# A two-block transformer kernel: the norm factor's broadcast earlier, the modulation's products later, first sums in PSUM

## The chip, the cores and the metric

The kernel runs on one core of a Trainium2 chip. The metric is the device time of one execution in microseconds (us). TensorE is called PE in the rows, VectorE DVE, ScalarE ACT, GpSimd POOL; SP issues the DMAs of the weights.

## The reference

x has 512 tokens of 1024 features, in fp32. Two blocks run one after the other. Each is a feed-forward part (2816 wide, gated with silu), a token mixer, and a second feed-forward part. What matters here is the first part of the first block, and the modulation that the second block takes from a vector c:

```python
def _rmsnorm(x, g):
    y = x * rsqrt(mean(x * x, axis=-1) + EPS)
    return y * g
h = _rmsnorm(x, ffn1_norm);  x = x + 0.5 * _swiglu(h, ffn1_w_gate, ffn1_w_up, ffn1_w_down)
h = _rmsnorm(x, mix_norm);   proj = h @ w_in            # then attention and retention on proj
...
h = _rmsnorm(x, ffn2_norm);  x = x + 0.5 * _swiglu(h, ffn2_w_gate, ffn2_w_up, ffn2_w_down)
# second block, before its first sublayer:
mod = silu(c) @ w_ada + b_ada                           # 1024 x 9216
```

## The kernel before

**Layout and units.** x is kept feature-major: 8 tiles of 128 features x 512 tokens. All weights come in one stream of units, each of 128 x 1024 fp32, through a ring of four (`raw`). ACT makes the rounded high part of a unit (`act_split`, L223), POOL the low part (`pool_split`, L230), into `split`, also a ring of four. TensorE takes three matmuls for each 128x128 tile, high by high, high by low, low by high (`three_passes`, L243): 24 matmuls for a unit. A unit is split up to three units ahead of TensorE (LOOKAHEAD) and loaded up to four ahead of its split. A semaphore `unit_used` counts units that TensorE has finished, `unit_lo` units that POOL has split.

**Late norm.** Three norms, those before a.ffn1, a.in and a.ffn2, are "late": the matmuls run on x times the gain, and the factor 1/rms of each token is applied to the result. While the first units run, the squares of x are added up over the 8 tiles (ACT squares at L584, DVE adds at L577). TensorE then sums over partitions with one-column matmuls (`pe_mean_square`, L254, 16 matmuls), ACT takes the root (L290), DVE the reciprocal (L304) and a diagonal (L284), TensorE spreads it over all partitions (`pe_rows`, L279), and ACT copies that "factor" to SBUF (L298). DVE multiplies each finished bank by it (L535 and L544 in the FFN, L716 in the projection). Four PSUM banks serve the units of a group of four, so the first unit of the next group waits until the first bank has been scaled.

**The projection a.in.fm** has five groups of four units, numbered here 0 to 19; unit 4 is the first of the second group. Beside it, DVE makes the modulation: w_ada comes in 8 chunks of 8 tiles (128 x 1152). For each tile DVE multiplies by an entry of silu(c) and adds into one accumulator (`dve_ada`, first tile of a chunk L816, the others L819). TensorE sums each finished chunk over partitions with 9 fp32 matmuls, each of two passes, so 18 in the trace (`pe_ada`, L834), and DVE adds the bias (L825). The next chunk's first product waits for those sums.

**SP's order.** Weight units and w_ada tiles are issued by SP's one queue, in the order of the code (L785 to L804, with ADA_TILES = ((0, 1, 2), (3, 4, 5), (6, 7), ())). The ring for w_ada has four slots. So tile 4 waits until tile 0 has been added, and everything behind it in SP's program waits too:

```python
            if tile >= 4:
                nc.sync.wait_ge(sem("ada_added"), tile - 3)
...
            for u in range(4):
                self.sp_unit(name, t, u)
                if u > 1:
                    self.sp_ada(chunk0 + t, u - 2)
            for u in (2, 3):
                self.sp_ada(chunk0 + t, u)
```

For the first group that gives: units 0, 1, 2, tiles 0, 1, 2, unit 3, tiles 3 to 7, then units 4, 5, 6, tiles 8 to 10, unit 7, tiles 11 to 15, unit 8. Every wait is written out by hand; `meet` (L193) is a barrier of the engines between stages. The functions that the change touches follow, with what calls them.

Of the kernel before, what the change touches and what calls it, by code (L numbers as in the profile page):

```python
# [11 lines left out]
ALU = mybir.AluOpType  # L12
# [7 lines left out]
KD = D // P  # L20
# [9 lines left out]
LOOKAHEAD = 3  # L30
# [34 lines left out]
class Signals:  # L65
# [7 lines left out]
    def sem(self, name):  # L73
        if name not in self.sems:
            self.sems[name] = self.stack.enter_context(self.nc.semaphore(name))
        return self.sems[name]

    def to(self, name, *event, by=1):
        self.count[name] = self.count.get(name, 0) + by
        assert (name, event) not in self.made, (name, event)  # L80
        self.made[name, event] = self.count[name]
        return by

    def at(self, name, *event):
        if self.known is None:
            return 1
        return self.known[name, event]


class Kernel:  # L90
# [354 lines left out]
    def pe_ffn(self, pre, in_front=None):  # L445

        nc, sem, to, at = self.nc, self.sem, self.to, self.at
        late = pre in self.LATE
        free = ("gate_scaled", "up_scaled") if late else ("silu", "act_mul")
        first, last = self.plan[pre + ".up"]["unit"], self.plan[pre + ".up"]["n"] - 1  # L450
        for t, u, g in self.units(pre + ".up"):
            if t > 0:
                nc.tensor.wait_ge(sem(free[u % 2]), at(free[u % 2], pre, t - 1, u // 2))
            elif in_front:
                nc.tensor.wait_ge(sem("resid"), at("resid", in_front, 4 + u))
            nc.tensor.wait_ge(sem("unit_lo"), g + 1)
            for j in range(KD):
                if g == first:
                    self.pe_hs_ready(pre, j)
                mm = self.three_passes(self.ps[:, u, :], slice(j * P, (j + 1) * P), self.hs[:, 0, j, :],  # L460
                                       self.hs[:, 1, j, :], g % RING, j == 0, j == KD - 1)
            mm.then_inc(sem("unit_used"), 1)
            if late and g == first + 1 + (pre == "a.ffn1"):
                self.pe_mean_square(pre)
            if late and g == first + 3:
                self.pe_rows(pre, 7, self.rs)
        for t, u, g in self.units(pre + ".down"):
            mt, part = u // 3, u % 3
            if part == 0 and t == 0:
                nc.tensor.wait_ge(sem(free[mt % 2]), at(free[mt % 2], pre, last, mt // 2))  # L470
            if part == 0 and t > 0:
                nc.tensor.wait_ge(sem("resid"), at("resid", pre, (t - 1) * 4 + mt))
            nc.tensor.wait_ge(sem("unit_lo"), g + 1)
            k0 = sum(DOWN_TILES[:part])
            for j in range(DOWN_TILES[part]):
                if t == 0 and mt == 0:
                    nc.tensor.wait_ge(sem("act_lo"), at("act_lo", pre, (k0 + j) // 2, (k0 + j) % 2))
                mm = self.three_passes(self.ps[:, mt, :], slice(j * P, (j + 1) * P), self.a_s[:, 0, k0 + j, :],
                                       self.a_s[:, 1, k0 + j, :], g % RING, k0 + j == 0, k0 + j == KF - 1)
            mm.then_inc(sem("unit_used"), 1)  # L480
# [184 lines left out]
    def pe_fm_tile(self, g, bank, src, k_from=0, k_n=KD, ready=None):  # L665
# [4 lines left out]
                                   src[1][:, j, :], g % RING, j == 0, j == k_n - 1)  # L670
        return mm

    def pe_fm_project(self, name, n, hook=None):
        nc, sem, to, at = self.nc, self.sem, self.to, self.at
        late = n in self.LATE
        for t, u, g in self.units(name):
            if t > 0:
                e = "fm_dve" if late or u % 2 == 1 else "fm_act"
                nc.tensor.wait_ge(sem(e), at(e, name, t - 1, u))
            elif late:  # L680
                nc.tensor.wait_ge(sem("resid"), at("resid", "a.ffn1", 4 + u))
            nc.tensor.wait_ge(sem("unit_lo"), g + 1)
            self.pe_fm_tile(g, u, self.h_parts, ready=n if t == 0 and u == 0 else None).then_inc(sem("unit_used"), 1)
            if late and t == 0 and u == 1:
                self.pe_mean_square(n)
            if late and t == 0 and u == 3:
                self.pe_rows(n, 7, self.rs)
            if hook and u == 3:
                hook(t)

    def act_fm_project(self, name, dst, late=False):
        nc, sem, to, at = self.nc, self.sem, self.to, self.at
        for t, u, g in self.units(name):
            if not (late and t == 0 and u in (1, 2)):
                self.act_split(g + LOOKAHEAD)
            if late and t == 0 and u == 0:
                self.act_split(g + LOOKAHEAD + 1)
                self.act_rstd("a.in")
                self.act_split(g + LOOKAHEAD + 2)
                self.act_rs("a.in", self.rs_in[:, :])  # L700
            if not late and u % 2 == 0:
                nc.scalar.wait_ge(sem("unit_used"), g + 1)
                nc.scalar.activation(dst[:, 4 * t + u, :], self.ps[:, u, :], ACT.Copy).then_inc(
                    sem("fm_act"), to("fm_act", name, t, u))

    def dve_fm_project(self, name, dst, hook=None, late=False):
        nc, sem, to, at = self.nc, self.sem, self.to, self.at
        if late:
            hook(0, 0)
            hook(0, 1)  # L710
            self.dve_rstd("a.in", self.col_in)
            nc.vector.wait_ge(sem("rs"), at("rs", "a.in"))
        for t, u, g in self.units(name):
            if late:
                nc.vector.wait_ge(sem("unit_used"), g + 1)
                nc.vector.tensor_tensor(dst[:, 4 * t + u, :], self.ps[:, u, :], self.rs_in[:, :], ALU.mult).then_inc(  # L716
                    sem("fm_dve"), to("fm_dve", name, t, u))
            elif u % 2 == 1:
                nc.vector.wait_ge(sem("unit_used"), g + 1)
                nc.vector.tensor_copy(dst[:, 4 * t + u, :], self.ps[:, u, :]).then_inc(  # L720
                    sem("fm_dve"), to("fm_dve", name, t, u))
            if hook and not (late and t == 0 and u < 2):
                hook(t, u)

    def pe_tm_project(self, name, width, hook=None):
# [1411 lines left out]
            self.act_square(n, j, self.x[:, j, :])  # L2137

    def dve_start(self):
        nc, sem, to = self.nc, self.sem, self.to  # L2140
        n, gain = "a.ffn1", self.vec(0)
        nc.vector.memset(self.ones[:, :], 1.0)
        nc.vector.memset(self.eps, EPS)
        nc.vector.memset(self.ssq[:, :], 0.0).then_inc(sem("ssq"), to("ssq", n, -1))
        nc.vector.wait_ge(sem("vecs_landed"), 16)
        for j in range(KD):
            if j % 2 == 0:
                nc.vector.wait_ge(sem(f"x_landed{j // 2}"), 16)
            self.dve_late_lo(n, gain, j)
        for j in range(KD):  # L2150
            self.dve_into_ssq(n, j)
        nc.vector.wait_ge(sem("ident_landed"), 16)

    def act_tables(self, *tables):
# [429 lines left out]
```

## Time and profile before

| what | value |
|---|---|
| median of 3 runs | 2935.22 us (2931.61 to 2938.62) |
| the profiled execution | 2931.5 us |
| its span | 2930.2 us |
| mean granted TensorE clock | 0.949 of full |
| TensorE matmul busy | 2707.9 us, 92% |
| weight unit loads (512 KB), median from issue to landing | 3.4 us |
| w_ada tile loads (576 KB), the same | 5.8 us |

The profile is one execution, taken by the hardware. Its span runs from the first to the last recorded instruction. Rows of a timeline merge equal instructions that follow each other: start, length of the merged stretch, engine, line, tiles, count, and in brackets how long the engine was idle before and what ended that. A matmul counts as busy until its modelled end, so a busy TensorE is not one at its peak.

### The profile page before, as it was taken

Reading aid. Unit: us, or ns where it says so; the run is one execution under the profiler, and the core shown is the slowest. Engines: PE = TensorE matmul, PEld = TensorE weight load, DVE = VectorE, ACT = ScalarE, POOL = GpSimd, SP = SyncE. Lnnn points to the kernel's source line nnn. Section 1 sums busy time; section 2 is a strip of 40 time slices with the busy share of each in tenths; the row PEclk is TensorE's granted clock in tenths of the full one; section 3 lists DMA queues with packets and bytes.
Section 4 is the critical chain, followed back from the end, with each engine's and each line's share of the span. In section 5 each row is a group of like instructions: output and inputs, shape, how many; then the busy total and the mean of one; then the engine's idle time right before and its main releaser. Section 6 shows DMA issues by size and latency. Waiting matters only on the chain.

```text
span 2930.2 us, 30093 instructions
## 1 busy us (share of the span) xinstructions
PE 2707.9 (92%) x12126; PEld 2159.6 (74%) x12126; DVE 868.3 (30%) x1425; ACT 931.4 (32%) x1497; POOL 1270.0 (43%) x645
## 2 busy tenths in 40 slices
PE   8999999975699899999999999998977699899998
PEld 7888878744466688788888788887855487788886
DVE  4222146543666311322211311102026423311101
ACT  4233211202455422332322322223246423322221
POOL 4444434412477344444444444444433344444443
PEclk9999999976799999999999999998989799899999
DMA  4222257712000122222322223231210022132321
GB/s 157 95 99 90 90 206 281 267 40 73 7 1 1 65 94 94 87 94 94 100 93 95 79 94 97 91 96 62 94 49 1 6 96 86 52 100 95 98 92 61
DMA packets 75754, 261.48 MB, mean 89 GB/s; under 512 B 9184, under 2 KB 10464, under 8 KB 75616
## 3 DMA queue, kind: packets, MB, share of 16 engines
q1 hardware_dynamic: 72368, 255.45, 26.3%
q10 hardware_dynamic: 3248, 4.12, 0.5%
q8 instruction: 96, 1.57, 0.2%
q14 instruction: 42, 0.34, 0.0%
HBM read 257.44 MB, written 2.10 MB: 89 GB/s over the span
## 4 chain that ended last, share of the span: by engine, by line
PE 66%; DVE 4%; POOL 3%; ACT 2%; issue 1%; DMA 0%; ACTq 0%; POOLq 0%; DVEq 0%
PE ps L243 57%; POOL prob L1419 2%; PE ps L254 1%; PE ps L1218 1%; PE ps L1575 1%; PE ps L1188 1%; PE ps L1175 1%; PE ps L1176 0%; PE ps L1540 0%; PE ps L279 0%; POOL prob_d L1866 0%; PE ps L1564 0%; ACT hs L431 0%; PE ps L1225 0%; PE ps L1541 0%
## 5 line engine op out<-in xcount | busy, mean ns | idle before, releaser
L230 POOL TENSOR_TENSOR split_ring<-raw_ring,split_ring 128x1024 fp32r<-128x1024 f32 x416 | 1006.2, 2422 | 1301.8 <-ACT split_ring L223 1301.7
L243 PE MATMUL ps<-hs,split_ring 128*128 128x512 f32 x6240 | 1439.6, 392 | 34.8 <-DVE hs L333 8.9
L243 PEld LDWEIGHTS ps<-hs,split_ring 128*128 128x128 f32 x6240 | 1179.9, 189 | 293.4 <-issue 14.7
L223 ACT ACTIVATE split_ring<-raw_ring 128x1024 fp32r<-128x1024 f32 x416 | 437.2, 1052 | 559.6 <-PE ps L243 393.0
L243 PE MATMUL ps<-ffn_act,split_ring 128*128 128x512 f32 x2112 | 495.4, 396 | 0.0
L243 PEld LDWEIGHTS ps<-ffn_act,split_ring 128*128 128x128 f32 x2112 | 397.8, 188 | 97.0
L512 ACT ACTIVATE ffn_act<-tmp 128x512 fp32r<-128x512 f32 x88 | 55.6, 632 | 385.2 <-DVE tmp L548 385.2
L1419 POOL TENSOR_SCALAR prob<-prob,small 128x512 f32<-128x512 f32 (+3 forms) x128 | 140.4, 1115 | 59.7 <-DVE small L1463 59.7
L548 DVE TENSOR_TENSOR tmp<-ps,tmp 128x512 f32<-128x512 f32 x44 | 30.4, 691 | 380.6 <-PE ps L243 380.6
L243 PE MATMUL ps<-split_ring,hs 128*128 128x512 f32 (+1 forms) x480 | 106.1, 384 | 10.3 <-POOLq L196 7.9
L243 PEld LDWEIGHTS ps<-split_ring,hs 128*128 128x128 f32 x480 | 88.9, 197 | 26.5 <-POOLq L196 8.1
L819 DVE SCALAR_TENSOR_TENSOR ada_acc<-ada_w,c_silu,ada_acc 128x1152 f32<-128x1152 f32 x56 | 88.3, 1578 | 9.2 <-DMA ada_w<-in_w_ada 4.8
L544 DVE TENSOR_TENSOR tmp<-ps,sq 128x512 f32<-128x512 f32 x44 | 30.4, 690 | 184.4 <-PE ps L243 184.4
L551 DVE TENSOR_TENSOR ffn_act<-tmp,ffn_act 128x512 fp32r<-128x512 f32 x88 | 64.5, 733 | 61.4 <-ACT ffn_act L512 61.4
L617 DVE SCALAR_TENSOR_TENSOR x<-ps,x 128x512 f32<-128x512 f32 x24 | 16.6, 691 | 221.9 <-PE ps L243 221.9
L633 DVE TENSOR_SCALAR y_over_hs<-ps,coef 128x512 f32<-128x512 f32 x16 | 12.0, 750 | 224.7 <-ACT sq L584 224.7
L2062 DVE TENSOR_TENSOR tmp<-tmp,ps 128x512 f32<-128x512 f32 x32 | 21.3, 684 | 186.1 <-PE ps L243 186.1
L1218 PE MATMUL ps<-turned,vg 128*64 128x512 f32 (+3 forms) x256 | 73.9, 442 | 0.7 <-ACT turned L1376 0.7
L1368 ACT ACTIVATE prob<-ps,small 128x512 f32<-128x512 f32 (+3 forms) x128 | 65.7, 529 | 20.2 <-DVE small L1446 13.3
L509 ACT ACTIVATE tmp<-ps 128x512 f32<-128x512 f32 x44 | 26.3, 598 | 131.6 <-PE ps L243 131.5
L509 ACT ACTIVATE tmp<-tmp 128x512 f32<-128x512 f32 x44 | 27.8, 632 | 123.6 <-DVE tmp L535 123.6
L535 DVE TENSOR_TENSOR tmp<-ps,sq 128x512 f32<-128x512 f32 x44 | 30.4, 690 | 114.7 <-PE ps L243 97.5
(294 smaller groups left out, 2451.7 us busy)
## 6 DMA issues: line engine op xcount, KB each, us to landing
raw_ring<-in_wstream SPq DMA_DIRECT2D x380, 512.0 KB, 3.4
ada_w<-in_w_ada SPq DMA_DIRECT2D x64, 576.0 KB, 5.8
raw_ring<-in_wstream SPq DMA_DIRECT2D x32, 384.0 KB, 3.0
x<-in_x_t SPq DMA_DIRECT2D x4, 512.0 KB, 6.6
decay<-in_decay ACTq DMA_DIRECT2D x4, 512.0 KB, 3.6
out_t<-x SPq DMA_DIRECT2D x8, 256.0 KB, 2.0
raw_ring<-in_wstream SPq DMA_DIRECT2D x4, 304.0 KB, 5.8
cos_r<-in_cos_r ACTq DMA_DIRECT2D x1, 256.0 KB, 3.6
```

What stands on the lines that cost most here:

```text
L223: nc.scalar.activation(self.split[:, s, 0, :], self.raw[:, s, :], ACT.Copy).then_inc(self.sem("unit_hi"), 1)
L230: nc.gpsimd.tensor_tensor(self.split[:, s, 1, :], self.raw[:, s, :], self.split[:, s, 0, :].bitcast(F32), ALU.subtract).then_inc(self.sem( ...
L243: mm = self.nc.tensor.matmul(out, lhs, rhs, start=first and j == 0, stop=last and j == 2)
L509: nc.scalar.activation(self.tmp[:, f, :], gate, ACT.Silu).then_inc(sem("silu"), to("silu", pre, t, f))
L512: nc.scalar.activation(self.a_s[:, 0, 2 * t + f, :], self.tmp[:, 2 + f, :], ACT.Copy).then_inc(sem("act_hi"), to("act_hi", pre, t, f))
L535: nc.vector.tensor_tensor(self.tmp[:, f, :], self.ps[:, u, :], self.rs, ALU.mult).then_inc(sem("gate_scaled"), to("gate_scaled", pre, t, f))
L544: nc.vector.tensor_tensor(up, self.ps[:, u, :], self.rs, ALU.mult).then_inc(sem("up_scaled"), to("up_scaled", pre, t, f))
L551: nc.vector.tensor_tensor(self.a_s[:, 1, 2 * t + f, :], self.tmp[:, 2 + f, :], self.a_s[:, 0, 2 * t + f, :].bitcast(F32), ALU.subtract).th ...
L819: i = nc.vector.scalar_tensor_tensor(self.ada_acc[:, :], w, self.c_silu[:, j:j + 1], self.ada_acc[:, :], ALU.mult, ALU.add)
L1218: mm = nc.tensor.matmul(self.ps[64 * g:64 * g + 64, 7, kb * P:T], self.vg[:, kb, 2 * kind + g, 0:DH], self.pt_n[:, kind, (self.PT_AT + P) ...
L1368: e = nc.scalar.activation(self.prob_n[:, kind, dst:dst + n], self.ps[:, i, col:col + n], ACT.Exp, bias=self.small[:, k:k + 1], scale=-1.0 ...
L1419: s = nc.gpsimd.tensor_scalar(x, x, self.small[:, 16 + k:17 + k], None, ALU.mult)
```

## The change

- In both late FFN stages the factor's broadcast (`pe_rows`) stands behind the third unit instead of the fourth. In a.ffn1 the mean square stands behind the second unit instead of the third; in a.ffn2 it already did.
- In a.in.fm the broadcast stands behind the third unit too. The sums of chunk 0 stand behind unit 5 (group 1, u = 1) instead of unit 3, those of chunk 1 behind unit 8 instead of unit 7; from chunk 2 on nothing changes.
- DVE's first six products no longer stand ahead of the reciprocal; each follows the scaling of its own unit, behind the factor.
- ACT splits units 4 and 5 behind the root and the factor's copy, one with each unit, instead of ahead of them.
- At the start of a.ffn1 the running sum of squares is in PSUM bank 6; only the last add writes to SBUF.

```diff
--- before.py
+++ after.py
@@ -460,9 +460,9 @@
                 mm = self.three_passes(self.ps[:, u, :], slice(j * P, (j + 1) * P), self.hs[:, 0, j, :],
                                        self.hs[:, 1, j, :], g % RING, j == 0, j == KD - 1)
             mm.then_inc(sem("unit_used"), 1)
-            if late and g == first + 1 + (pre == "a.ffn1"):
+            if late and g == first + 1:
                 self.pe_mean_square(pre)
-            if late and g == first + 3:
+            if late and g == first + 2:
                 self.pe_rows(pre, 7, self.rs)
         for t, u, g in self.units(pre + ".down"):
             mt, part = u // 3, u % 3
@@ -670,6 +670,8 @@
                                    src[1][:, j, :], g % RING, j == 0, j == k_n - 1)
         return mm
 
+    ADA_LATER = {(1, 1): 0, (2, 0): 1}
+
     def pe_fm_project(self, name, n, hook=None):
         nc, sem, to, at = self.nc, self.sem, self.to, self.at
         late = n in self.LATE
@@ -683,20 +685,19 @@
             self.pe_fm_tile(g, u, self.h_parts, ready=n if t == 0 and u == 0 else None).then_inc(sem("unit_used"), 1)
             if late and t == 0 and u == 1:
                 self.pe_mean_square(n)
-            if late and t == 0 and u == 3:
+            if late and t == 0 and u == 2:
                 self.pe_rows(n, 7, self.rs)
-            if hook and u == 3:
+            if hook and late and (t, u) in self.ADA_LATER:
+                hook(self.ADA_LATER[t, u])
+            if hook and u == 3 and not (late and t < 2):
                 hook(t)
 
     def act_fm_project(self, name, dst, late=False):
         nc, sem, to, at = self.nc, self.sem, self.to, self.at
         for t, u, g in self.units(name):
-            if not (late and t == 0 and u in (1, 2)):
-                self.act_split(g + LOOKAHEAD)
+            self.act_split(g + LOOKAHEAD)
             if late and t == 0 and u == 0:
-                self.act_split(g + LOOKAHEAD + 1)
                 self.act_rstd("a.in")
-                self.act_split(g + LOOKAHEAD + 2)
                 self.act_rs("a.in", self.rs_in[:, :])
             if not late and u % 2 == 0:
                 nc.scalar.wait_ge(sem("unit_used"), g + 1)
@@ -706,8 +707,6 @@
     def dve_fm_project(self, name, dst, hook=None, late=False):
         nc, sem, to, at = self.nc, self.sem, self.to, self.at
         if late:
-            hook(0, 0)
-            hook(0, 1)
             self.dve_rstd("a.in", self.col_in)
             nc.vector.wait_ge(sem("rs"), at("rs", "a.in"))
         for t, u, g in self.units(name):
@@ -719,7 +718,7 @@
                 nc.vector.wait_ge(sem("unit_used"), g + 1)
                 nc.vector.tensor_copy(dst[:, 4 * t + u, :], self.ps[:, u, :]).then_inc(
                     sem("fm_dve"), to("fm_dve", name, t, u))
-            if hook and not (late and t == 0 and u < 2):
+            if hook:
                 hook(t, u)
 
     def pe_tm_project(self, name, width, hook=None):
@@ -2137,18 +2136,22 @@
             self.act_square(n, j, self.x[:, j, :])
 
     def dve_start(self):
-        nc, sem, to = self.nc, self.sem, self.to
+        nc, sem, to, at = self.nc, self.sem, self.to, self.at
         n, gain = "a.ffn1", self.vec(0)
         nc.vector.memset(self.ones[:, :], 1.0)
         nc.vector.memset(self.eps, EPS)
-        nc.vector.memset(self.ssq[:, :], 0.0).then_inc(sem("ssq"), to("ssq", n, -1))
+        nc.vector.memset(self.ps[:, 6, :], 0.0).then_inc(sem("ssq"), to("ssq", n, -1))
         nc.vector.wait_ge(sem("vecs_landed"), 16)
         for j in range(KD):
             if j % 2 == 0:
                 nc.vector.wait_ge(sem(f"x_landed{j // 2}"), 16)
             self.dve_late_lo(n, gain, j)
-        for j in range(KD):
-            self.dve_into_ssq(n, j)
+        for j in range(KD - 1):
+            nc.vector.wait_ge(sem("squared"), at("squared", n, j))
+            nc.vector.wait_ge(sem("ssq"), at("ssq", n, j - 1))
+            total = self.ps[:, 6, :]
+            nc.vector.tensor_tensor(self.ssq[:, :] if j == KD - 2 else total, self.sq[:, j % 2, :], total,
+                                    ALU.add).then_inc(sem("ssq"), to("ssq", n, j))
         nc.vector.wait_ge(sem("ident_landed"), 16)
 
     def act_tables(self, *tables):
```

`sp_ada` and `sp_ada_stage` are the same in both kernels.

## Rows read from the trace of the kernel before

**Rows 1.** The page, part 1: busy time of each engine, share of the span, instructions.
```profile
PE 2707.9 (92%) x12126; PEld 2159.6 (74%) x12126; DVE 868.3 (30%) x1425; ACT 931.4 (32%) x1497; POOL 1270.0 (43%) x645
```

**Rows 2.** Timeline of a.ffn1's start: start, us, engine, line, what, [idle before <-releaser].
```profile
13.33 5.21 POOL L230 TENSOR_TENSOR split_ring<-raw_ring,split_ring 128x1024 fp32r<-128x1024 f32 x2 [5.11 <-ACT split_ring L223]
...
15.08 7.98 DVE L577 TENSOR_TENSOR ssq<-ssq,sq 128x512 f32<-128x512 f32 x7 [1.67 <-ACT sq L584]
...
19.91 0.63 ACT L584 ACTIVATE sq<-x 128x512 f32<-128x512 f32 x1 [0.16 <-DVE ssq L577]
...
26.93 0.95 PE L254 MATMUL ps<-ones,ssq 128*128 128x1 f32 x8
...
34.20 1.02 PE L279 MATMUL ps<-sq,ones 128*128 128x512 f32 x2
...
36.63 23.68 PE L243 MATMUL ps<-hs,split_ring 128*128 128x512 f32 x103 [1.41 <-DVE tmp L535]
...
42.38 7.64 POOL L230 TENSOR_TENSOR split_ring<-raw_ring,split_ring 128x1024 fp32r<-128x1024 f32 x3 [9.88 <-ACT split_ring L223]
...
45.25 0.68 DVE L535 TENSOR_TENSOR tmp<-ps,sq 128x512 f32<-128x512 f32 x1
...
48.61 1.95 DVE L548 TENSOR_TENSOR tmp<-tmp 128x512 f32<-128x512 f32 x1
```

**Rows 3.** Timeline of a.ffn2's first units.
```profile
1258.89 0.69 DVE L284 TENSOR_TENSOR sq<-ident,tiny 128x512 f32<-128x512 f32 x1
...
1271.65 28.63 PE L243 MATMUL ps<-hs,split_ring 128*128 128x512 f32 x125 [1.41 <-DVE tmp L535]
```

**Rows 4.** Timeline of a.in.fm, its first four units and the first sums.
```profile
382.00 0.82 DVE L816 TENSOR_SCALAR ada_acc<-ada_w,c_silu 128x1152 f32<-128x1152 f32 x1 [1.47 <-DMA ada_w<-in_w_ada]
383.57 2.94 DVE L819 SCALAR_TENSOR_TENSOR ada_acc<-ada_w,c_silu,ada_acc 128x1152 f32<-128x1152 f32 x2 [0.75 <-DMA ada_w<-in_w_ada]
...
390.70 11.17 PE L243 MATMUL ps<-hs,split_ring 128*128 128x512 f32 x48
391.39 1.46 SPq L208 DMA_DIRECT2D raw_ring<-in_wstream  x3
...
396.61 1.06 ACT L223 ACTIVATE split_ring<-raw_ring 128x1024 fp32r<-128x1024 f32 x1 [9.29 <-DMA raw_ring<-in_wstream]
397.57 0.24 ACT L290 ACTIVATE tiny<-ps,tiny 128x4 f32<-128x4 f32 x1
397.75 5.17 POOL L230 TENSOR_TENSOR split_ring<-raw_ring,split_ring 128x1024 fp32r<-128x1024 f32 x2 [7.97 <-ACT split_ring L223]
...
402.77 0.60 ACT L298 ACTIVATE rs_in<-ps 128x512 f32<-128x512 f32 x1 [3.79 <-PE ps L279]
...
409.52 4.00 PE L834 MATMUL ps<-ones,ada_acc 128*128 128x1 f32 x18 [6.79 <-DVE ada_acc L819]
```

**Rows 5.** Timeline of a.in.fm around unit 8; the first line from a shorter stretch.
```profile
427.57 1.41 DVE L819 SCALAR_TENSOR_TENSOR ada_acc<-ada_w,c_silu,ada_acc 128x1152 f32<-128x1152 f32 x1
...
426.96 0.69 DVE L716 TENSOR_TENSOR pqr<-ps,rs_in 128x512 f32<-128x512 f32 x1 [0.98 <-PE ps L243]
...
429.38 1.38 SPq L208 DMA_DIRECT2D raw_ring<-in_wstream  x3
...
436.43 7.06 POOL L230 TENSOR_TENSOR split_ring<-raw_ring,split_ring 128x1024 fp32r<-128x1024 f32 x3 [19.22 <-ACT split_ring L223]
...
437.64 2.06 PE L834 MATMUL ps<-ones,ada_acc 128*128 128x1 f32 x18
...
463.71 22.05 PE L243 MATMUL ps<-hs,split_ring 128*128 128x512 f32 x96 [0.20 <-POOL split_ring L230]
```

**Rows 6.** PE by stretch: us, busy (instructions), granted clock, DMA share, GB/s.
```profile
413.40:418.40 5.00, 5.00 (x13) 0.50 0.15 59
...
515.40:520.80 5.40, 5.40 (x21) 0.50 0.64 207
...
537.60:541.30 3.70, 3.70 (x9) 0.50 0.53 166
```

## The prediction

> **What bounds the kernel now.** I read the page first: TensorE is busy for 2707.9 of 2930.2 us [rows 1], so time moves only where TensorE waits, does extra work, or runs at its lower clock. Then PE's waits in the stages that the diff touches, then their timelines, where the same waits stand in brackets. They show three places:
>
> - In a.ffn1 the broadcast of the factor (L279) stands behind unit 3, the stage's fourth. Rows end at 35.22, ACT copies them, DVE scales the first bank, and only then may TensorE take unit 4: it sits idle 1.41 us before 36.63 [rows 2].
> - a.ffn2 has the same gap, 1.41 us before 1271.65 [rows 3].
> - In a.in.fm the broadcast ends at 402.7 and the first modulation sums (L834) wait 6.8 us for DVE's products, then take 4.00 us for 18 matmuls where the same 18 take 2.06 later [rows 4, 5]. The granted clock, which had been full, was 0.50 (1.2 of 2.4 GHz) in 413.4:418.4 [rows 6], after that idle time. Unit 4 starts at 413.4.
>
> The reader should also see two chains here. ACT's square root at 397.57 comes 7 us after the mean square, since it is queued behind the split of unit 4, whose data landed at 396.6 [rows 4]. And SP is one ordered queue: unit 4's load, issued at 391.39 [rows 4], stands behind the load of product tile 7, which waits until tile 3 has been added. Unit 8's load likewise stands behind tile 15, which waits for tile 11.
>
> **The change, part by part.** One unit of 24 matmuls is a quarter of the 22.05 us that 96 took at 463.71: 5.5 us [rows 5].
>
> *First sums in PSUM, mean square behind the second unit (a.ffn1).* TensorE had used 17.8 us for three units up to 26.9; unit 2 takes 5.5 of it, so unit 1 ends at 21.4. The sums must be done by then. Before, the seven adds ran from 15.08 to 23.06 [rows 2]. Squares and adds alternate at one per 0.79 us when nothing disturbs them (0.63 and 0.16 idle [rows 2]). The first adds fell beside POOL's splits (13.33 to 18.54): at the undisturbed pace the seventh would have ended near 20.4. An operation that reads PSUM took 0.68 at 45.25 with POOL splitting from 42.38 to 50.02 [rows 2]. If the new adds are like that, squares 2 to 7 run at 0.79 from 15.85 and end at 20.4: no wait. If they pace as before, TensorE waits until 23.1, 1.7 us. I take none, by the row at 45.25, which is the nearest in form. The memset of a PSUM bank stands where the other stood, at DVE's idle start: nothing. The Trainium skill ("SBUF — State Buffer", section "SBUF: two separate sides") says that VectorE and GpSimd hold a shared port pair for a whole instruction when the VectorE one has two SBUF inputs; this trace agrees (the multiplication of two SBUF tiles at 48.61 took 1.95 us beside the same POOL run [rows 2]). By that rule the sums are ready at 20.4, without it at 23.1.
>
> *Rows behind the third unit (a.ffn1, a.ffn2).* The diagonal must be ready when unit 2 ends. In a.ffn2 it is ready at 1259.6 [rows 3] and unit 2 ends at 1263.7. In a.ffn1 the mean square would run 21.4 to 23.3; root (0.24 [rows 4]), reciprocal and diagonal (0.69 [rows 3]) need about 1.1 us, and unit 2 ends at 28.8. The rows then cost their same 1.02 us, and the copy (0.60) and scaling (0.69) lie beside unit 3. The idle 1.41 us goes, twice: -2.8. What is late next is nothing within 5 us: the weights of units 4 and 5 are split ahead in this stage as before.
>
> *No extra splits ahead, products delayed (a.in.fm).* Nothing changes until the mean square, 388.8 to 390.7. Now root, reciprocal and diagonal follow at once, ready by 392.1. Unit 2 ends at 390.7 + 5.5 = 396.2, rows until 397.2, ACT's copy (0.60) until 397.9. Unit 3 ends at 397.2 + 5.5 = 402.8. Up to here everything has cover.
>
> But DVE has not done its first products. Before, tile 0 ran at 382.0 and tiles 1 and 2 at 383.57 [rows 4], while DVE had nothing else. Now they come behind the factor. From 397.9: scale bank 0 (0.69) to 398.6; tiles 0 to 2, 0.82 + 2.94, to 402.3; scale bank 1 to 403.0; tile 3 (1.41 [rows 5]) to 404.4. Only then does SP pass tile 7 (0.4) and issue unit 4, at 404.8 instead of 391.4. With two or three product loads in front, that unit landed 5.2 us after its issue (391.39 to 396.61 [rows 4]): 410.0. ACT's split 1.1, POOL's 2.4: 413.6. TensorE had been free since 402.8. The new idle time is 10.8 us, and unit 4 starts at 413.6 where it started at 413.4: the old wait is exchanged for another, +0.2. Bounds: the landing may take 3.4 us (the median of these loads, in the table of the page) or 5.9 (429.38 to 436.43 less ACT's 1.1 [rows 5]) and some, say 6.9 with four product loads in front, so -1.6 to +1.9. The clock falls in both cases during this idle time; I take the same half-speed stretch after the restart, 5 us [rows 6].
>
> The first sums are not saved either, they move behind unit 5: +2.06 [rows 5].
>
> Then unit 8. Chunk 1's first product waits for these sums to have been read. Let E be the end of unit 5 (426.9 before [rows 5]). Sums to E + 2.06, DVE's bias add to E + 2.3, scale bank 0 to E + 2.9, tiles 8 to 10 to E + 6.8, scale bank 1 to E + 7.5, tile 11 to E + 8.9. In the old run tile 11 began at 427.57, so it ended at 429.0, unit 8's load went out at 429.38, and POOL had split it by 436.43 + 7.06 / 3 = 438.8 [rows 5]: 9.8 us after the tile. So now the weights are ready at E + 18.7. TensorE is ready at E + 2.06 + 11.0 = E + 13.1 (it used to be there at 437.64 + 2.06 = 439.7, 0.9 after the weights: there was little room). New idle time: +5.6, with the bounds 3.8 to 7.5 from the same landing times.
>
> An idle stretch of 5.6 us also costs clock. The row 515.40:520.80 is such a place: TensorE had waited 3.8 us at a meeting of the engines, then ran at 0.50 for 5.4 us of full work [rows 6]; half of that is lost, 2.7, and 1.9 at 537.6:541.3, after a wait of 4.2. I take +2.4, between 0 and 2.8. The Trainium skill ("TensorE: Matmul & The Clock Gate", "What's actually happening") says that the array is throttled by default and activity releases it; by that rule too the wait costs more than its own length, by the other view it would be +5.6 alone.
>
> From unit 12 on the sums stand where they stood, behind a chunk's last unit, and the chain tile, load, split again fits: with F the end of unit 8, its weights are ready at F + 19.5 and TensorE, sums included, at F + 20.6. It was just as tight before (0.20 idle on POOL at 463.71 [rows 5]). Nothing is given back there.
>
> **Sum.** -1.4 - 1.4 + 0.2 + 2.1 + 5.6 + 2.4 = +7.5 us. The profiled execution took 2931.5 (span 2930.2); 2939.0 on its own scale. It lies at the low end of the three runs (2931.61 to 2938.62), so I put the sum on their median: 2935.2 + 7.5 = 2942.7.
>
> **Rivals.**
> 1. *The loads aren't held (faster).* If unit 4's and unit 8's loads ran far enough ahead, TensorE would go from unit 3 straight on: 402.8 instead of 413.4, -10.6; sums +2.1; clock never lost, -2.6; with -2.8, -13.9: 2921.3. It decides at one point: unit 4's load must go out before 394. For it speaks that unit 4's weights were ready at 400.3 before (POOL 397.75 and 2.6 [rows 4]) and that both visible waits of the old stage vanish. Against it speaks SP's order, which the diff leaves alone.
> 2. *Only the first stall is real.* If unit 8 comes in time (DVE 3 us faster and a landing of 3.4), the sum is +0.2 + 2.1 - 2.8 = -0.5: 2934.7.
> 3. *The sums at the start are late.* +1.7 at unit 1, and the gain in a.ffn1 is used up: 2944.4.
> 4. *The clock is kept through the second wait*: 2940.3; or it stays low for one stretch like the first wherever it falls, another +1.7.
>
> **How the numbers follow.** Forecast with rival 4: 0.72, own range 2938 to 2947 (the landing bounds, both ways, and the clock). Rival 1: 0.08; rival 2: 0.12; rival 3: 0.05; anything else 0.03. The range that leaves out 2 in 10 is 2933 to 2948, the runs' own scatter of 3 us included. A change of 0.2%, 5.9 us, is about what a measurement tells from none; so slower begins at 2941.1. Of the forecast and rival 3 about three quarters lie above: 0.58. Same: the rest of these and rival 2, 0.32. Faster: rival 1 and a little, 0.10.
>
> **What would show it.** In the changed kernel's trace: PE waits in a.in.fm for POOL's split before unit 4 (about 10.8 us) and again before unit 8 (about 5.6), and no longer for ada_acc; the raw load of unit 4 issued 27 us after the stage's first matmul instead of 13.5; ACT's copy of the factor at 19 us instead of 25; no idle time before unit 4 in either FFN; the first adds at 0.69 each. A stage a.in.fm that is 10 us longer and two FFN stages each 1.4 shorter would confirm the sum. It is wrong if unit 4 starts less than 30 us after the stage's first matmul (35.7 by the sum), or if unit 4's load doesn't stand behind tile 7 in SP's queue.

## The result

| kernel | median | runs | profiled execution (span) |
|---|---|---|---|
| before | 2936.04 us | 8 (2931.61 to 2938.62) | 2931.5 (2930.2) |
| changed | 2943.34 us | 8 (2941.31 to 2946.36) | 2942.45 (2941.1) |

The ratio is 1.0028, 95% interval 1.0018 to 1.0037: the change makes the kernel 7.3 us slower. The forecast was 2942.7 us, +7.5. The page of the changed kernel, its span and busy times, against [rows 1]:

```profile
span 2941.1 us, 30093 instructions
...
PE 2710.9 (92%) x12126; PEld 2161.0 (73%) x12126; DVE 858.5 (29%) x1425; ACT 932.2 (32%) x1497; POOL 1271.1 (43%) x645
```

PE does 3 us more of busy time in a span 10.9 us longer. What it waits for in a.in.fm, the stretch 370 to 525 (us in total, times, longest):

```profile
PE ps L243 <- POOL split_ring L230: 18.8, 2, 12.9
```

The wait for ada_acc (6.79 us [rows 4]) is gone. Two waits for POOL's split stand in its place, 18.8 us together.

**The FFN stages.** The timeline of a.ffn1's start, against [rows 2], and then the two rows of a.ffn2 against [rows 3]:

```profile
14.57 4.70 DVE L2153 TENSOR_TENSOR ps<-sq,ps 128x512 f32<-128x512 f32 x6 [1.20 <-ACT sq L584]
...
19.38 0.69 DVE L2153 TENSOR_TENSOR ssq<-sq,ps 128x512 f32<-128x512 f32 x1
...
21.85 0.95 PE L254 MATMUL ps<-ones,ssq 128*128 128x1 f32 x8
...
24.31 1.93 DVE L284 TENSOR_TENSOR sq<-ident,tiny 128x512 f32<-128x512 f32 x1
...
29.13 1.02 PE L279 MATMUL ps<-sq,ones 128*128 128x512 f32 x2
...
29.58 10.59 PE L243 MATMUL ps<-hs,split_ring 128*128 128x512 f32 x44
```

```profile
1274.89 1.02 PE L279 MATMUL ps<-sq,ones 128*128 128x512 f32 x2
...
1275.35 24.86 PE L243 MATMUL ps<-hs,split_ring 128*128 128x512 f32 x107
```

The seven adds end at 20.07 instead of 23.06, the mean square starts at 21.85 without a wait, and unit 3 follows the broadcast at once. Unit 4 has no row of its own, since TensorE never stopped there: the 1.41 us of [rows 2] and [rows 3] are gone in both stages. The diagonal took 1.93 us beside POOL (0.69 was the figure used), with 3 us to spare.

**a.in.fm up to unit 4**, the timeline against [rows 4]:

```profile
376.77 11.06 PE L243 MATMUL ps<-hs,split_ring 128*128 128x512 f32 x48
...
389.54 0.26 ACT L290 ACTIVATE tiny<-ps,tiny 128x4 f32<-128x4 f32 x1 [3.50 <-PE ps L254]
...
396.00 0.60 ACT L298 ACTIVATE rs_in<-ps 128x512 f32<-128x512 f32 x1 [6.19 <-PE ps L279]
...
397.23 0.81 DVE L815 TENSOR_SCALAR ada_acc<-ada_w,c_silu 128x1152 f32<-128x1152 f32 x1
398.16 2.94 DVE L818 SCALAR_TENSOR_TENSOR ada_acc<-ada_w,c_silu,ada_acc 128x1152 f32<-128x1152 f32 x2
...
401.61 4.46 DVE L818 SCALAR_TENSOR_TENSOR ada_acc<-ada_w,c_silu,ada_acc 128x1152 f32<-128x1152 f32 x3
403.42 1.88 SPq L208 DMA_DIRECT2D raw_ring<-in_wstream  x3
...
410.73 1.06 ACT L223 ACTIVATE split_ring<-raw_ring 128x1024 fp32r<-128x1024 f32 x1 [14.14 <-DMA raw_ring<-in_wstream]
...
411.87 7.00 POOL L230 TENSOR_TENSOR split_ring<-raw_ring,split_ring 128x1024 fp32r<-128x1024 f32 x3 [23.36 <-ACT split_ring L223]
...
414.36 13.46 PE L243 MATMUL ps<-hs,split_ring 128*128 128x512 f32 x48 [12.91 <-POOL split_ring L230]
```

The reader can follow the chain downwards. The root comes at 389.54, 12.8 us after the stage's first matmul (19.5 before); the factor at 396.0; then the first product at 397.23, where it had run at 382.0. SP issues unit 4 at 403.42, ACT can split it at 410.73, and TensorE, idle for 12.91 us, starts it at 414.36.

**Around unit 8**, against [rows 5]:

```profile
427.65 2.06 PE L833 MATMUL ps<-ones,ada_acc 128*128 128x1 f32 x18
...
431.35 2.94 DVE L818 SCALAR_TENSOR_TENSOR ada_acc<-ada_w,c_silu,ada_acc 128x1152 f32<-128x1152 f32 x2
...
434.81 4.46 DVE L818 SCALAR_TENSOR_TENSOR ada_acc<-ada_w,c_silu,ada_acc 128x1152 f32<-128x1152 f32 x3
436.62 1.75 SPq L208 DMA_DIRECT2D raw_ring<-in_wstream  x3
...
442.94 1.06 ACT L223 ACTIVATE split_ring<-raw_ring 128x1024 fp32r<-128x1024 f32 x1 [23.08 <-DMA raw_ring<-in_wstream]
...
446.57 7.34 PE L243 MATMUL ps<-hs,split_ring 128*128 128x512 f32 x24 [5.84 <-POOL split_ring L230]
...
474.19 22.03 PE L243 MATMUL ps<-hs,split_ring 128*128 128x512 f32 x96
```

The sums run to 429.7, tiles 9 and 10 from 431.35, tile 11 from 434.81; unit 8's load goes out at 436.62, has landed at 442.9 and is split by 446.4. TensorE had been free at 440.7: 5.84 us idle. The clock, in the columns of [rows 6] (us, PE busy, granted clock, DMA share, GB/s):

```profile
403.40:410.70 7.30, 0.00 (x0) 0.65 0.97 344
...
414.40:419.20 4.80, 4.80 (x12) 0.50 0.79 319
...
446.60:449.90 3.30, 3.30 (x8) 0.50 1.02 419
450.00:453.70 3.70, 3.70 (x17) 1.00 0.26 101
```

Both waits leave TensorE at 0.50 for some time after the restart: unit 8 takes 7.34 us where a unit at full clock takes 5.5. The first row is the stretch in which unit 4's data landed, with a DMA share of 0.97 at 344 GB/s.

### The profile page after: what moved, and what is told of

It reads as the page before. It is cut to its first block, busy times and chain, and to the rows that moved or that the text cites. A ratio compares the mean times of both kernels' runs of the same rounds, so it can differ in the third digit from the quotient of the medians.

```text
span 2941.1 us, 30093 instructions
## 1 busy us (share of the span) xinstructions
PE 2710.9 (92%) x12126; PEld 2161.0 (73%) x12126; DVE 858.5 (29%) x1425; ACT 932.2 (32%) x1497; POOL 1271.1 (43%) x645
## 3 DMA queue, kind: packets, MB, share of 16 engines
q1 hardware_dynamic: 72368, 255.45, 26.7%
## 4 chain that ended last, share of the span: by engine, by line
PE 65%; DVE 4%; POOL 3%; ACT 2%; issue 1%; DMA 0%; ACTq 0%; POOLq 0%; DVEq 0%
PE ps L243 56%; POOL prob L1418 2%; PE ps L254 1%; PE ps L1217 1%; PE ps L1574 1%; PE ps L1187 1%; PE ps L1174 1%; PE ps L1175 0%; PE ps L1539 0%; PE ps L279 0%; POOL prob_d L1865 0%; PE ps L1563 0%; ACT hs L431 0%; PE ps L1224 0%; PE ps L1540 0%
## 5 line engine op out<-in xcount | busy, mean ns | idle before, releaser
L243 PE MATMUL ps<-hs,split_ring 128*128 128x512 f32 x6240 | 1444.3, 393 | 49.5 <-POOL split_ring L230 18.8
```

The source lines that it names most:

```text
L243: mm = self.nc.tensor.matmul(out, lhs, rhs, start=first and j == 0, stop=last and j == 2)
```

## The experiments

Each was timed against the kernel before on the same chip; "before" is the median of those runs. Five to eleven runs each. The four medians of the kernel before lie within 0.6 us, so rows are also compared with each other and with the changed kernel's 2943.34.

| run | median | before | ratio (95%) |
|---|---|---|---|
| e1 FFN part alone | 2932.79 | 2935.50 | 0.9990 (0.9981 to 0.9999) |
| e2 a.in.fm part alone | 2945.29 | 2935.50 | 1.0040 (1.0026 to 1.0054) |
| e3 units ahead of tiles, all groups | 2941.14 | 2935.50 | 1.0018 (1.0010 to 1.0027) |
| e4 products ahead | 2931.94 | 2935.50 | 0.9985 (0.9976 to 0.9994) |
| e5 products ahead, sums behind unit 4 | 2920.75 | 2935.94 | 0.9951 (0.9938 to 0.9963) |
| e6 units ahead of tiles, once | 2936.37 | 2935.94 | 1.0002 (0.9993 to 1.0011) |
| e7 sums behind unit 4 | 2938.21 | 2935.94 | 1.0004 (0.9995 to 1.0013) |
| e8 sums of squares in SBUF | 2945.05 | 2935.94 | 1.0034 (1.0022 to 1.0047) |
| e9 kernel before, sums behind unit 4 | 2928.59 | 2936.11 | 0.9974 (0.9962 to 0.9985) |
| e10 e1 with sums behind unit 4 | 2924.49 | 2936.11 | 0.9961 (0.9948 to 0.9974) |

**e1 and e2: the change in two halves.** Edits: the kernel before with `pe_ffn` and `dve_start` of the changed one (e1); the changed kernel with these two of the kernel before (e2).

> Of the change only the two FFN stages: broadcast behind the third unit, mean square of a.ffn1 behind the second, first sums in PSUM; a.in.fm as before. Theory A (the sum of the prediction: 1.4 us of idle time gone in each FFN stage, nothing given back): 2.8 us under the kernel before, 2933.2 if that is 2936.0. Rival (the idle time comes back elsewhere in the FFN): 0. A also expects no PE wait on DVE before unit 4 in either stage.

> Of the change only the stage a.in.fm: broadcast behind the third unit, no splits ahead, products behind the factor, first sums behind units 5 and 8. Theory A: waits of 12.9 and 5.8 us before units 4 and 8 as in the changed kernel, a stage 11 to 12 us longer, time 10 to 12 us over the kernel before (about 2947). Rival (the stages interact, the shift of 1.4 us matters to the loads): under 8.

e1 came out 2.7 us faster, with an interval that just leaves out 1, and PE has no wait on DVE before unit 4 in either FFN stage. e2 came out 9.8 slower, a little under what A expected, above the rival. Its waits of PE in a.in.fm:

```profile
PE ps L243 <- POOL split_ring L230: 18.0, 2, 12.1
```

-2.7 and +9.8 make +7.1; the whole change measured +7.3. The halves add.

**e3: SP's order in all groups** (the order in short, not the code).

```diff
+ for t in range(5):
+     units (t,0), (t,1), (t,2)
+     tiles 4..7 of chunk t-1, tiles 0..2 of chunk t
+     unit (t,3), tile 3 of chunk t
```

> The changed kernel with one edit: in a.in.fm SP issues units 0 to 2 of a group ahead of tiles 4 to 7 of the chunk before, so no weight unit stands behind a tile that waits for DVE's first products. DVE's and ACT's orders are those of the changed kernel. Theory A (SP's order holds units 4 and 8): both waits of PE (12.9 and 5.8 us) go and the clock stays high (another 4 us), 2943.3 - 22 = 2921. Rival B (the delayed products themselves or ACT's later splits are the cost): PE then waits for ada_acc or for ACT's split instead, gain under 10 us, 2934 or more.

Measured 2941.1, a miss by 20 us, and inside what the rival named. Both long waits for POOL's split did go (0.4 us is left), so SP's order did hold the two units. But PE now waits for ada_acc, 8.6 us in four waits, and the clock falls behind each of the four. The timeline shows one reason:

```profile
398.45 9.63 POOL L230 TENSOR_TENSOR split_ring<-raw_ring,split_ring 128x1024 fp32r<-128x1024 f32 x3 [9.24 <-ACT split_ring L223]
...
398.99 6.83 DVE L832 SCALAR_TENSOR_TENSOR ada_acc<-ada_w,c_silu,ada_acc 128x1152 f32<-128x1152 f32 x2
...
415.84 2.44 PE L847 MATMUL ps<-ones,ada_acc 128*128 128x1 f32 x18 [2.69 <-DVE ada_acc L832]
```

POOL splits units 4 to 6 from 398.45 to 408.1, and two products beside it take 6.83 us; they took 2.94 where POOL was silent. A second reason is likely, but only argued: the edit puts tiles 4 to 7 of every chunk three units later in SP's queue, in groups that had no need of it. e6 leaves those groups alone.

**e6: the same order, in the first group alone** (in short again).

```diff
- unit 3, tiles 3 4 5 6 7, units 4 5 6, tiles 8 9 10
+ unit 3, tile 3, units 4 5 6, tiles 4 5 6 7 8 9 10
```

> The changed kernel; SP issues units 4, 5 and 6 ahead of tiles 4 to 7, in the first group alone, and keeps its order after that. Theory A: the wait before unit 4 (12.9 us) goes, but POOL's splits of units 4 to 6 now run beside DVE's first products, which take longer for it (as in e3, where two took 6.8 us instead of 2.9), so the first sums wait some 3 us for ada_acc; the wait before unit 8 stays near 5.8: 2943.3 - 11 = 2932. Rival B (only the delayed products count, SP's order is innocent): 2940 or more.

```profile
379.60 1.46 SPq L208 DMA_DIRECT2D raw_ring<-in_wstream  x3
...
397.73 9.63 POOL L230 TENSOR_TENSOR split_ring<-raw_ring,split_ring 128x1024 fp32r<-128x1024 f32 x3 [9.03 <-ACT split_ring L223]
...
398.27 6.83 DVE L828 SCALAR_TENSOR_TENSOR ada_acc<-ada_w,c_silu,ada_acc 128x1152 f32<-128x1152 f32 x2
...
415.13 3.24 PE L843 MATMUL ps<-ones,ada_acc 128*128 128x1 f32 x18 [2.69 <-DVE ada_acc L828]
...
437.13 8.63 PE L243 MATMUL ps<-hs,split_ring 128*128 128x512 f32 x24 [5.59 <-POOL split_ring L230]
```

Unit 4's load went out at 379.60, and units 3, 4 and 5 run in one stretch from 395.51: the 12.9 us wait goes with SP's order alone, DVE's being that of the changed kernel. The first sums then wait 2.69 us for products slowed by POOL, and the wait before unit 8 stays (5.59). 2936.4 against 2932 expected: 7 us gained, not 11. The expectation had counted no clock loss at the first remaining wait; the sums took 3.24 us there instead of 2.06 and units 6 and 7 13.31 instead of 11.15. A third loss came behind a wait of only 0.33 us: units 12 to 15 took 23.64 us instead of 22.05. Against e3, the other groups in their old order are worth some 5 us.

**e4: products ahead of the reciprocal again.**

```diff
+            hook(0, 0)
+            hook(0, 1)
             self.dve_rstd("a.in", self.col_in)
...
-            if hook:
+            if hook and not (late and t == 0 and u < 2):
                 hook(t, u)
```

> The changed kernel, but DVE makes the first six products ahead of the reciprocal, as in the kernel before; SP's order is untouched. Theory A: tile 3 is added near the end of unit 1, so unit 4 is loaded some 13 us after the stage's start and the first wait (12.9 us, and 2.6 of clock) goes, while the one before unit 8 (5.8, and 1.8 of clock) stays, since it hangs on the first sums standing behind unit 5: 2943.3 - 15 = 2928. Rival B (ACT without splits ahead is too late for unit 4): a wait of 2 to 8 us before unit 4 stays, 2933 or more.

```profile
391.02 1.46 SPq L208 DMA_DIRECT2D raw_ring<-in_wstream  x3
...
395.79 16.93 PE L243 MATMUL ps<-hs,split_ring 128*128 128x512 f32 x72
...
431.95 8.19 PE L243 MATMUL ps<-hs,split_ring 128*128 128x512 f32 x24 [6.31 <-POOL split_ring L230]
...
460.75 23.65 PE L243 MATMUL ps<-hs,split_ring 128*128 128x512 f32 x96 [0.35 <-POOL split_ring L230]
```

Unit 4 is loaded at 391.02 and follows unit 3 without a gap, though ACT no longer splits ahead; rival B falls. The second wait is still there, 6.31 us, and unit 8 ran slowly for 8.19. 2931.9 was measured where 2928 was expected, 11.4 under the changed kernel. The expectation left unit 8 as it was; it lost more (0.5 us of wait, 0.9 of clock), and units 12 to 15 took 1.6 us more than at full clock, behind a wait of 0.35.

**e7: the other wait alone.**

```diff
-    ADA_LATER = {(1, 1): 0, (2, 0): 1}
+    ADA_LATER = {(1, 0): 0, (1, 3): 1}
```

> The changed kernel with the first sums behind unit 4 and those of chunk 1 behind unit 7, nothing else. Theory A: the first wait (12.9 us, before unit 4) stays, the second (5.8 us) and its clock loss (1.8) go: 2943.3 - 7.5 = 2936. Rival (the second wait follows from the first, the loads being late by the same backlog): it stays, 2942 or more.

```profile
413.00 7.36 PE L243 MATMUL ps<-hs,split_ring 128*128 128x512 f32 x24 [11.19 <-POOL split_ring L230]
...
422.12 16.60 PE L243 MATMUL ps<-hs,split_ring 128*128 128x512 f32 x72
```

The first wait stays (11.19 us; unit 4's load landed in 5.58 us here). Units 5 to 7 run from 422.12, the sums for chunk 1 from 438.56, and unit 8 follows at 440.48 without idle time; a wait of 1.1 us appears before unit 16 instead. The time, 2938.2 against 2936 expected, lies 5.1 under the changed kernel. Its eleven runs spread over 11 us and the profiled one is among the fastest (2933.07), so A and its rival are told apart by the trace rather than by the median.

**e5: both.** e4 with the edit of e7.

> The kernel of e4 (products ahead of the reciprocal) with the first sums behind unit 4 instead of unit 5, and those of chunk 1 behind unit 7. Theory A (the wait before unit 8 hangs on where the first sums stand): chunk 1 begins 5.5 us earlier against the units, the 6.3 us wait before unit 8 shrinks to 1 or less and its clock loss goes: e4's 2931.9 - 8 = 2924. Rival (unit 8 is late by DMA rate, whatever DVE does): the wait stays at 4 us or more, 2930 or more.

```profile
395.49 11.49 PE L243 MATMUL ps<-hs,split_ring 128*128 128x512 f32 x48
...
406.82 2.06 PE L835 MATMUL ps<-ones,ada_acc 128*128 128x1 f32 x18
...
408.74 16.60 PE L243 MATMUL ps<-hs,split_ring 128*128 128x512 f32 x72
...
416.91 1.66 SPq L208 DMA_DIRECT2D raw_ring<-in_wstream  x3
...
427.19 22.05 PE L243 MATMUL ps<-hs,split_ring 128*128 128x512 f32 x96
```

From 395.49 on TensorE has no wait in the stage: units 3 and 4, sums, units 5 to 7, sums, unit 8, all at full clock. The load for unit 8 goes out at 416.91, in time. Two products beside POOL's splits took 6.29 us here too, but the first three had been made earlier, and the sums found all of them done. 2920.75 us, 3 under the expectation, 22.6 under the changed kernel and 15.2 under the kernel before: the fastest of these versions.

**e8: the port.** The changed kernel with `dve_start` of the kernel before.

> The changed kernel with the running sum of squares at the start in SBUF again. Theory A (adds with two SBUF inputs stand behind POOL's splits, adds with one in PSUM do not): the adds end near 22.6 instead of 20.1 us, TensorE waits some 1.5 us for them behind unit 1 and the kernel is slower by that, 2944.8. Rival (the adds were in time anyway): no wait, 2943.3.

```profile
14.86 8.48 DVE L577 TENSOR_TENSOR ssq<-ssq,sq 128x512 f32<-128x512 f32 x7 [1.12 <-ACT sq L584]
...
23.39 1.05 PE L254 MATMUL ps<-ones,ssq 128*128 128x1 f32 x8 [0.52 <-DVE ssq L577]
```

The adds take 8.48 us instead of 5.5 and end at 23.3. The direction is right, but PE's wait is 0.52, not 1.5, as unit 1 ended at 22.9 in this execution. The median is 1.7 over the changed kernel's; that is inside the spread of both, so the PSUM edit's own worth is shown in the adds and only probable in the time.

**e9 and e10: where the kernel before could have gone.** One edit to each, in `pe_fm_project`:

```diff
+            if hook and late and (t, u) == (1, 0):
+                hook(0)
-            if hook and u == 3:
+            if hook and u == 3 and not (late and t == 0):
                 hook(t)
```

> The kernel before with one edit: the first sums stand behind unit 4 instead of unit 3 (products ahead of the reciprocal, splits ahead, broadcast behind the fourth unit, as before). Theory A: the wait of 6.8 us for ada_acc is covered by unit 4, the sums take 2.06 instead of 4.00 us and unit 4 runs at the full clock (2.6 more); the idle 1.4 us before unit 4 for the first scaled bank appears in exchange: 2936 - 10 = 2926. Rival (unit 8's load comes no earlier, so the wait moves there): 2933 or more.

> The kernel of e1 (the FFN part of the change alone) with the edit of e9: first sums behind unit 4. Against e5 (2920.8) it lacks the broadcast behind the third unit in a.in.fm and ACT's later splits. Theory A (the two gains add): e9 - 2.8, near 2923, and 1.4 to 3 over e5. Rival (e5's products and splits only fit each other): 2928 or more.

e9 gains 7.5 us of the 10 expected. PE's waits in a.in.fm, besides the meetings, then the row of units 8 to 11 and the clock at its start:

```profile
PE ps L243 <- DVE pqr L718: 1.4, 1, 1.4
PE ps L243 <- POOL split_ring L230: 1.3, 2, 0.7
...
431.35 23.68 PE L243 MATMUL ps<-hs,split_ring 128*128 128x512 f32 x96 [0.70 <-POOL split_ring L230]
...
431.40:434.80 3.40, 3.40 (x10) 0.62 0.98 394
```

The 6.8 us are covered, the 1.4 us for the first scaled bank appear as expected, and 1.3 us for the splits of units 8 and 12, 0.7 and 0.6: the chain from the sums to the next group's weights is about as long as the group itself. The first of these waits also costs clock: units 8 to 11 take 23.68 us instead of 22.05. These 1.3 and 1.6 us are what is missing from the 10. e10 adds the FFN part, 4.1 us less than e9 (2.8 expected). It lies 3.7 over e5 (1.4 to 3 expected), which has the earlier broadcast in a.in.fm as well; what e10 has and e5 has not is the wait of 1.4 for the first scaled bank and, before unit 8, a wait of 0.35 with 1.6 of clock.

## Why the prediction was right

Terms of the sum against the profile of the changed kernel:

| step | predicted | measured |
|---|---|---|
| a.ffn1, idle before unit 4 | -1.4 | -1.4 (no wait left) |
| a.ffn2, the same | -1.4 | -1.4 |
| start of unit 4, from the stage's first matmul | +0.2 | +2.3 (37.59 against 35.3) |
| clock after the wait before unit 4 | as before | as before (2.3 lost, 2.4 before) |
| first sums behind unit 5 | +2.1 | +1.9 |
| wait before unit 8 | +5.6 | +5.84 |
| clock after that wait | +2.4 | +1.8 (7.34 against 5.5) |

- *The two gates in SP's queue.* Right in place and cause. Unit 4's load went out 26.7 us after the stage's first matmul (27 said), ACT's copy of the factor came at 19.2 (19), unit 8's load at E + 9.0 (E, the end of unit 5, is 427.6), its weights were ready at E + 18.8 (18.7). The first wait needs two things at once, as the prediction said: the products behind the factor, and the weights behind the products' tiles in SP's queue. e4 takes away the one, e6 the other, and the wait goes each time; both keep ACT's later splits, so those did not cause it. e7 shows that the place of the sums makes the second wait.
- *The landing of unit 4 was mis-sized.* 5.2 us were taken from the old load; it took 7.31 (403.42 to 410.73), above the 6.9 named as the upper end. The wait before unit 4 was therefore 12.9 us, not 10.8. The kernels of e2, e7 and e8 have the same orders up to unit 4 and issue these loads at the same distances: there it took 6.52, 5.58 and 6.75 us, and the waits were 12.1, 11.2 and 12.4. So 7.31 is the longest of four executions, and all four lie above 5.2. Before, SP's tiles 4 to 7 had gone out over 8 us; now products run without pause and the four loads go out at 1.5 to 1.9 us distance. That this lengthens the landing is argued, not shown, and it doesn't explain the spread: e7, with the same distances, had a DMA share of 0.96 at 356 GB/s.
- *The wait before unit 8* came out by two small errors that cancel: tile 11 was added at E + 8.6, not 8.9, and the load took 6.3 us, not 5.9. Its bounds, 3.8 to 7.5, don't follow from the landing times named; from 5.9 down to 3.4 and up to 6.9 they are 3.1 to 6.6. (In the same way unit 4's start is 35.5 us by the sum, 413.6 less 378.1, and not 35.7.)
- *The sum.* The measured terms give +9.0, not +7.5. Those inside a.in.fm make +11.8, and unit 12 does begin 11.8 us later, counted from the stage's first matmul (97.4 against 85.6). The profiled executions differ by 10.9; the other 1.9 us arise where the code is the same, and no cause is shown for them. The medians differ by 7.3, with runs that scatter over 7 us before and 5 us after. The place and the cause of each wait were foreseen, and every size to about 2 us; that +7.5 meets +7.3 to 0.2 is luck.
- *Rival 1* (no load held) falls by the waits themselves. It is close to what e5's edits make of the kernel: 15.2 us under the kernel before, where 13.9 were worked out. *Rival 2* (only the first stall) is e7's situation: +2.3 us there, where -0.5 was worked out. *Rival 3* (late sums) falls: no wait at unit 1. *Rival 4* (clock kept) falls: 0.50 in 446.6:449.9.
- *The port.* The adds at 0.78 each beside POOL's splits, against 8 us for seven with SBUF sums (e8), agree with the Trainium skill ("SBUF — State Buffer", "SBUF: two separate sides"). The first adds took a step of 0.78 us, not the 0.69 named. The prediction didn't draw from the same rule that the products, which read two SBUF tiles, slow down beside POOL too. In the changed kernel that cost nothing, since POOL had stood idle for 23.36 us up to 411.87; e3 and e6 paid for it.

## What to carry to other kernels

When work is moved behind a wait, list every load that the same in-order DMA queue holds for it: here TensorE never waited for the products, and the weights queued behind their buffers cost 13 us. A slow chain (sums, products, buffer free, load, split) must be started as early as its inputs allow, even a unit before TensorE would otherwise need it: one unit earlier was worth 7.5 us in the kernel before. And a fix of the order of loads can bring two engines to work side by side that slow each other: e3 and e6 lost a part of what they had won that way.

## What was not expected of the hardware

- Two products of 1.42 us each took 6.83 us together while POOL split three units (9.63 us), and POOL's three splits took 9.63 instead of 7.0: both engines lose. The two works alone make 2.9 + 7.0 = 9.9 us, so the stretch is about as long as if the engines had taken turns (an estimate).
- One 512 KB load behind four of 576 KB, all issued at the same distances, landed in 5.58, 6.52, 6.75 and 7.31 us in four executions, where such loads take 3.4 in the median. What makes the difference between the four is open.
- A short wait can cost more clock than its own length. Behind 2.06 us of sums and a wait of 0.33 to 0.70 us, the next four units took 23.6 to 23.7 us instead of 22.05 in e4, e6, e9 and e10, with a granted clock of 0.53 to 0.62 in the first 3.3 us. But the kernel before (0.20, at 463.71), e6 before unit 16 (0.69) and e7 (1.11) stood behind the same sums and kept the full clock. The length of the wait does not tell the two cases apart.
